# Modulation weights in column halves, attention values by query halves, two late recurrence levels on alternating column groups, and two pieces of sample work in later places, in a one-core decoder layer

## The chip, the cores and the metric

The kernel runs on one core of a Trainium2 chip. The metric is the device time of one execution in microseconds (us), lower is better. The time before is the median of three executions.

## The reference

One layer of a hybrid decoder runs over a prompt of 2048 tokens and over 8 sample rows, all in fp32, width 1024. What matters here, shortened:

```python
mod = c @ w_ada + b_ada                       # conditioning, 9 rows (8 samples and the prompt)
shift, scale, gate = split(mod, 3)
h = rms_norm(x, norm_g) * (1 + scale) + shift
qa, ka, va, za, qb, fb, ib, zb = split(h @ w_in)
# A: attention in a window of 128 keys, two key/value groups, heads of 64
p = softmax(qa @ k.T * d**-0.5 masked to 0 <= rel < 128, with sinks)
ya = (p @ v) * silu(za)
# B: gated linear recurrence over chunks, 4 heads of 128
S_new = exp(Lc) * S + (k * exp(Lc - L)).T @ v
o = (q * exp(L)) @ S + (A = decayed causal q k.T) @ v
yb = rms_norm(o) * silu(zb)
y = g_a * (ya @ w_proj_a) + g_b * (yb @ w_proj_b)
out = x + gate * (y @ w_out)
```

A query sees its own block of 128 keys up to itself and the part of the previous block that is less than 128 keys back. So of the previous block the second half of the queries (64 to 127) needs only keys 64 to 127, and of its own block the first half of the queries (0 to 63) needs only keys 0 to 63.

## The kernel before

The prompt is done in four iterations `it` of 512 tokens. Each is a fixed list `UNITS` of 68 dense units. A unit is one PSUM bank of results, made of 24 matmuls (12 for `pa` and `pb`): each fp32 product is three matmuls of split values (`w_hi` with `h_hi`, `w_hi` with `h_lo`, `w_lo` with `h_hi`). Units alternate between the banks `D0` and `D1`, and a unit has two halves, `hf_` 0 and 1. TensorE (PE) does `dense(it, u, hf_)` and then the side tasks that the table `SIDE` holds for this place, in the order in which `put` and `at_half` wrote them (`at_half(it, n, ..)` is unit n // 2, half n % 2). The other engines go through the same table in the same order. VectorE (DVE) in one half first does "early" tasks (`PV`, `norm` in half 1), then the evacuation of the unit, then the rest. Everything waits by semaphores; the banks `XA` to `XD` are handed round by counts (`full`, `freed`, `free`).

The side tasks that matter here, in an iteration:

- `S`, `norm`, `PT`, `PV` (units 9 to 19): the attention in eight pieces of 128 queries by 2 x 2 heads. `PV` multiplies the transposed weights `PT` by the values `vtok`: for two key blocks and two groups one matmul of 256 columns, results of 64 partitions each. It is 32 bursts in the whole kernel, each recorded as 8 matmuls, since the profile has an fp32 matmul as two.
- `dg` (unit 20): the products of the recurrence in blocks of 32 on the diagonal, 64 matmuls (128 records); DVE then multiplies `qq` by `ff` and takes the diagonal.
- `level` 0 to 6 (from unit 21 on, one per unit): products between blocks of 1, 2, .. 64 tokens. Level 5 is 32 matmuls of 32 result partitions and 32 columns, on column groups 0 and 2 of the array in turn (64 records); level 6 is 16 matmuls of 64 result partitions and 64 columns, all on the first column group (32 records). DVE copies the results to `AT`. `KT`, `o` and `st` follow in units 28 to 31; `KT` waits for DVE's last product of level 6 (`lvl`), `o` for its copy.
- In iteration 1 the sample rows' recurrence: `vB` and `so` (units 1 to 9), `srms` (DVE, unit 26) and `soss` (unit 27): PE transposes what `srms` scaled, and `XC` is used by `soss` and `KT` in turn.
- Five DVE instructions for the sample rows (`esel`, `ib_hi`, `ib_lo`, clearing of `R3`, `qz_b`), called the esel block here, stand before unit 65 of iteration 0 (`NU - 3`) and wait there for the last low part of the next tile (`h_lo` 8).

Ahead of the iterations is the prologue. SyncE (SP) issues all loads on one queue: `w_ada` in eight loads of 128 rows x 2048 columns (shift and scale), the four tiles of x, small rows, then the first three weight blocks. PE multiplies `cT` (the 9 conditioning rows) by the `ada` tiles into four banks (`p_mod` counts pairs of tiles), DVE and ScalarE (ACT) copy the four banks to `mod_rows`, PE turns these rows into columns (32 records of 9 columns, L682), DVE makes `shift` and `gscale`, `modulate` makes h of a tile (8 DVE instructions, L1186), ACT its high part (L942) and GpSimd (POOL) its low part (L1588), and then unit 0 can begin. DVE's order is fixed:

```python
            s.wait_ge("p_mod", 4)
            s.done(cp(mod_rows[:, 0:512], pb["D0"][:, :]), "p_rows")
            s.done(cp(mod_rows[:, 1024:1536], XC[:, :]), "p_rows")
            s.wait_ge("p_T", 3)
```

Of the kernel before, what the change touches and what calls it, by code (L numbers as in the profile page):

```python
# [17 lines left out]
HB = 4  # L18
# [128 lines left out]
put(0, 0, 0, "xturn", 3)  # L147
for it in range(NIT):
# [28 lines left out]
    put(it, 20, 0, "dg", 0, "XA")  # L177
# [26 lines left out]
    if it == 1:  # L204
# [4 lines left out]
        put(1, 27, 0, "soss", 0, "XC")  # L209
# [21 lines left out]
for _it in range(NIT):  # L231
    for _u in UNITS:
        if _u in TH:
# [6 lines left out]
           "lvl", "at0", "smax", "p_exp", "p_norm", "kst", "on", "yf", "yh", "yl", "y7f", "y7h", "y7l", "x_in0", "x_in1", "xst", "rstd",  # L240
# [3 lines left out]
        + [f"ada{k}" for k in range(KT)] + [f"gw{p}" for p in range(4)]  # L244
        + ["p_late", "p_load0", "p_load1", "p_load2", "p_load3", "p_load4", "p_c", "p_T", "p_xs", "p_mod", "p_vec", "p_lb", "p_exp0", "p_rows", "p_scale", "p_x2",
           "p_x3", "p_bg", "fin", "act_step", "dve_step", "pool_step"])

# [51 lines left out]
def build(nc, A, O):  # L299

    ctx = ExitStack()
    with ctx:
# [186 lines left out]
        def _(sp):  # L489
# [10 lines left out]
            def ada_load(k):  # L500
                load(ada[k], A["w_ada"][0, P * k:P * k + P, 0:2 * D], f"ada{k}")

            ada_load(0), ada_load(1)
            load(x_p[0], x[0:P, :], "x_in0")
            load(x_p[1], x[P:2 * P, :], "x_in1")
# [5 lines left out]
            ada_load(2), ada_load(3)  # L511
            load(x_p[2], x[2 * P:3 * P, :], "p_x2")
            load(x_p[3], x[3 * P:4 * P, :], "p_x3")
            for k in range(4, KT):
                ada_load(k)
# [94 lines left out]
            for n in range(NRAW):  # L610
                weights(n)
            load(ones[:, :], A["c_ones"], "p_load2")
# [5 lines left out]
            for p in range(4):  # L618
                s.wait_ge("p_mod", (1, 2, 3, 3)[p])
                load(gate_w[p], A["w_ada"][0, 2 * P * p:2 * P * p + 2 * P, 2 * D:3 * D].rearrange(  # L620
                    "(k p) n -> p k n", p=P), f"gw{p}")
# [24 lines left out]
        def _(pe):  # L646
# [7 lines left out]
            for p in range(4):  # L654
                for k in (2 * p, 2 * p + 1):
                    s.wait_ge(f"ada{k}", 16)
                for n, b in enumerate(("D0", "D1", "XC", "XD")):
                    for k in (2 * p, 2 * p + 1):
                        r = slice(32 * (k % 4), 32 * (k % 4) + 32)
                        ins = mm(pb[b][r, :], cT[:, k, :], ada[k][:, 512 * n:512 * n + 512], start=k < 4, stop=k >= 4)  # L660
                s.done(ins, "p_mod")
                if p == 0:
                    s.wait_ge("p_load1", 16 * 6)
                    s.done(tr(XB[:, 512:512 + NV], vrow, ident[0:NV, 0:NV]), "p_T")
            s.wait_ge("p_vec", 1)
# [11 lines left out]
            s.wait_ge("p_rows", 4)  # L677
            s.wait_ge("p_xs", 1)
            for k in range(KT):
                tr(pb["D1"][:, NS * k:NS * k + NS], xs_row[:, P * k:P * k + P], ident[0:NS, 0:NS])  # L680
            for n in range(2 * KT):
                ins = mm(pb["D0"][:, 9 * n:9 * n + 9], mod_rows[:, P * n:P * n + P], sel, start=True, stop=True)  # L682
            s.done(ins, "p_T")
            x_turn(-1, 2, x_p[2])

            def dense(it, u, hf_):
# [4 lines left out]
                if hf_ == 0:  # L691
                    s.wait_ge(f"D{u % 2}_free", (it * NU + u) // 2)
                    s.wait_ge("w_lo", it * NB + blocks[-1] + 1)
                    if u < NT:
                        s.wait_ge("h_lo", 4 * it + u + 1)
                    if u == 1:
                        s.wait_ge("p_scale", 1)
# [26 lines left out]
            def side(it, task, a, key):  # L724
# [102 lines left out]
                elif task == "dg":  # L827
                    s.wait_ge("kk", 4 * it + 4)
                    s.unit_left(it, "qb", 3)
                    for n in range(16):  # L830
                        h, c = n // NT, P * (n % NT)
                        for g in range(4):
                            r = slice(c + 32 * g, c + 32 * g + 32)
                            ins = mm(bank[32 * g:32 * g + 32, 32 * n:32 * n + 32], kk[:, h, r], qq[:, h, r],
                                     start=True, stop=True)
                elif task == "level":
                    s.wait_ge("lvl", 8 * it + a + 1)
                    w = 2 ** a
                    for n in range(16):
                        h, c = n // NT, P * (n % NT)  # L840
                        for g in range(4) if a < 5 else (0, 2) if a == 5 else (0,):
                            r, left = slice(c + 32 * g, c + 32 * g + 32), 32
# [5 lines left out]
                            ins = mm(bank[32 * g:32 * g + left, m * n:m * n + m], kk[:, h, c + 32 * g:c + 32 * g + left],  # L848
# [69 lines left out]
        def _(act):  # L918
# [24 lines left out]

            s.wait_ge("x_in0", 16)
# [6 lines left out]
            squares(x_p[3], 3, srow[:, :])  # L951
            s.wait_ge("p_lb", 1)
            s.done(fn(lbt[:, 1:3, :], lbt[:, 1:3, :], ACT.Exp), "p_exp0")
            for t in range(NT):
                scale_x(-1, t, x_p[t])
            s.wait_ge("p_mod", 4)
            s.done(fn(mod_rows[:, 512:1024], pb["D1"][:, :], ACT.Copy), "p_rows")
            s.done(fn(mod_rows[:, 1536:2048], XD[:, :], ACT.Copy), "p_rows")
            for n in ATTACH[-1]:
                split_hi(n)  # L960
            h_high(-1, 0)
            h_high(-1, 1)
            h_high(-1, 2)
            h_high(-1, 3)
# [162 lines left out]
        def _(dve):  # L1127
# [53 lines left out]
            def modulate(it, t):  # L1181
                s.full(it, "xT", t)
                s.wait_ge("h_lo", 4 * (it + 1) + t - 1)
# [5 lines left out]

# [504 lines left out]
```

## Time and profile before

| | |
|---|---|
| median of 3 executions | 1648.69 us (1648.18 to 1651.08) |
| profiled execution | 1649.62 us, span of its instructions 1647.8 us |
| PE busy | 1610.2 us, 98% of the span |
| DVE, ACT, POOL busy | 763.6, 594.7, 830.3 us |
| TensorE's mean granted clock | 0.993 of 2.4 GHz |
| bytes moved | 172.6 MB, mean 105 GB/s |

PE is the engine that matters. Its busy time is the sum of times in which any matmul is under way, and a matmul of 512 columns shows as 0.39 us but the next begins 0.23 us after it. So what a burst costs is read from starts, not from sums. DVE, ACT and POOL have slack as averages; what they cost is read where PE waits for them. In the timeline a row is a group of like instructions: start, time from the first's start to the last's end, engine, line, names, partitions x columns, count, and in brackets the idle time before it with what ended it.

### The profile page before, as it was taken

Reading aid. Unit: us, or ns where it says so; the run is one execution under the profiler, and the core shown is the slowest. Engines: PE = TensorE matmul, PEld = TensorE weight load, DVE = VectorE, ACT = ScalarE, POOL = GpSimd, SP = SyncE. Lnnn points to the kernel's source line nnn. Section 1 sums busy time; section 2 is a strip of 40 time slices with the busy share of each in tenths; the row PEclk is TensorE's granted clock in tenths of the full one; section 3 lists DMA queues with packets and bytes.
Section 4 is the critical chain, followed back from the end, with each engine's and each line's share of the span. In section 5 each row is a group of like instructions: output and inputs, shape, how many; then the busy total and the mean of one; then the engine's idle time right before and its main releaser. Section 6 shows DMA issues by size and latency. Waiting matters only on the chain.

```text
span 1647.8 us, 31328 instructions
## 1 busy us (share of the span) xinstructions
PE 1610.2 (98%) x12840; PEld 1297.1 (79%) x12840; DVE 763.6 (46%) x1843; ACT 594.7 (36%) x1160; POOL 830.3 (50%) x1088
## 2 busy tenths in 40 slices
PE   6899999999999999999999999999999999999998
PEld 2687788877878777788878877888888977788887
DVE  2665444323558664522234764623346764633122
ACT  3335423334322551333432354243432354233330
POOL 1624433366664452446666353336677354346671
PEclk9899999999999999999999999999999999999999
DMA  8712212343545331233355232223455232123352
GB/s 315 214 53 85 70 41 65 90 128 105 173 131 131 103 90 35 71 92 114 103 168 139 54 92 63 63 69 115 128 169 162 66 89 66 54 67 88 94 164 72
DMA packets 299848, 172.62 MB, mean 105 GB/s; under 512 B 73646, under 2 KB 290055, under 8 KB 298664
## 3 DMA queue, kind: packets, MB, share of 16 engines
q1 hardware_dynamic: 299704, 170.61, 35.4%
q8 instruction: 102, 1.67, 0.4%
q14 instruction: 42, 0.34, 0.1%
HBM read 159.66 MB, written 11.96 MB: 104 GB/s over the span
## 4 chain that ended last, share of the span: by engine, by line
PE 68%; DVE 2%; issue 1%; ACT 0%; DVEq 0%
PE ps_D L720 39%; PE ps_D L717 18%; PE ps_XB L882 1%; PE ps_XB L876 1%; PE ps_XA L870 1%; PE ps_XB L848 1%; PE ps_XA L848 1%; PE ps_XB L895 1%; PE ps_XA L900 1%; PE ps_XB L894 1%; ACT p_or_hf L1064 0%; DVE p_or_hf L1416 0%; PE ps_XC L887 0%; PE ps_XC L785 0%; PE ps_XD L767 0%
## 5 line engine op out<-in xcount | busy, mean ns | idle before, releaser
L1580 POOL TENSOR_TENSOR w_lo_t<-w_raw,w_hi_t 128x256 fp32r<-128x256 f32 x928 | 680.7, 767 | 657.6 <-ACT w_hi_t L926 657.6
L720 PE MATMUL ps_D<-h_hi_t,w_hi_t 128*128 128x512 f32 x1024 | 415.1, 405 | 0.0
L720 PE MATMUL ps_D<-h_lo_t,w_hi_t 128*128 128x512 f32 x1024 | 401.1, 392 | 0.0
L720 PE MATMUL ps_D<-h_hi_t,w_lo_t 128*128 128x512 f32 x1024 | 400.1, 391 | 0.0
L926 ACT ACTIVATE w_hi_t<-w_raw 128x1024 fp32r<-128x1024 f32 x232 | 240.0, 1052 | 72.3 <-PE ps_D L717 39.3
L720 PEld LDWEIGHTS ps_D<-h_hi_t,w_hi_t 128*128 128x128 f32 x1024 | 192.3, 188 | 58.4 <-issue 21.2
L720 PEld LDWEIGHTS ps_D<-h_hi_t,w_lo_t 128*128 128x128 f32 x1024 | 192.3, 188 | 42.4
L720 PEld LDWEIGHTS ps_D<-h_lo_t,w_hi_t 128*128 128x128 f32 x1024 | 192.6, 188 | 35.8
L717 PE MATMUL ps_D<-w_hi_t,h_hi_t 128*128 128x384 f32 (+1 forms) x384 | 142.2, 370 | 2.7 <-POOL h_lo_t L1588 2.1
L717 PE MATMUL ps_D<-w_hi_t,h_lo_t 128*128 128x384 f32 (+1 forms) x384 | 136.6, 356 | 0.0
L717 PE MATMUL ps_D<-w_lo_t,h_hi_t 128*128 128x384 f32 (+1 forms) x384 | 136.6, 356 | 0.0
L717 PE MATMUL ps_D<-w_hi_t,y_hi_t 128*128 128x512 f32 x256 | 101.7, 397 | 2.1 <-DVE acc_t L1310 2.1
L717 PE MATMUL ps_D<-w_hi_t,y_lo_t 128*128 128x512 f32 x256 | 100.5, 393 | 0.0
L717 PE MATMUL ps_D<-w_lo_t,y_hi_t 128*128 128x512 f32 x256 | 100.3, 392 | 0.0
L989 ACT ACTIVATE th_t<-ps_D,bm_half 128x512 f32<-128x512 f32 x48 | 33.1, 689 | 143.5 <-PE ps_D L720 143.5
L717 PEld LDWEIGHTS ps_D<-w_hi_t,h_hi_t 128*128 128x128 f32 x384 | 72.7, 189 | 14.8 <-issue 8.4
L1292 DVE SCALAR_TENSOR_TENSOR acc_t<-th_t,ps_D 128x512 f32<-128x512 f32 x24 | 16.5, 688 | 140.5 <-PE ps_D L720 140.5
L1064 ACT ACTIVATE p_or_hf<-p_or_hf,sm 128x256 f32<-128x256 f32 x128 | 63.6, 498 | 45.6 <-DVE sm L1400 43.9
L717 PEld LDWEIGHTS ps_D<-w_lo_t,h_hi_t 128*128 128x128 f32 x384 | 72.7, 189 | 5.5
L717 PEld LDWEIGHTS ps_D<-w_hi_t,h_lo_t 128*128 128x128 f32 x384 | 72.8, 190 | 4.6
L1428 DVE SCALAR_TENSOR_TENSOR state<-state,ff,ps_XA 128x128 f32<-128x128 f32 x64 | 18.0, 343 | 117.2 <-PE ps_XA L900 117.2
L1350 DVE TENSOR_TENSOR qq<-qq,ff 128x1024 f32<-128x1024 f32 x28 | 37.6, 1345 | 72.1 <-PE ps_XB L848 45.5
(377 smaller groups left out, 2438.5 us busy)
## 6 DMA issues: line engine op xcount, KB each, us to landing
w_raw<-in_w_in SPq DMA_DIRECT2D x72, 512.0 KB, 3.9
w_raw<-in_w_merge SPq DMA_DIRECT2D x64, 512.0 KB, 4.0
w_raw<-in_w_in SPq DMA_DIRECT2D x64, 256.0 KB, 3.9
w_raw<-in_w_out SPq DMA_DIRECT2D x32, 512.0 KB, 4.1
x_or_AT<-in_x_prompt SPq DMA_DIRECT2D x20, 512.0 KB, 5.4
w_raw<-in_w_proj_a SPq DMA_DIRECT2D x64, 128.0 KB, 2.9
w_raw<-in_w_proj_b SPq DMA_DIRECT2D x32, 256.0 KB, 3.2
xr<-in_x_prompt SPq DMA_DIRECT2D x16, 512.0 KB, 5.1
```

The costliest lines, as they stand in the source:

```text
L717: ins = mm(bank[:, 0:P * nb].rearrange("p (n c) -> p n c", c=P), a[:, k, P * j:P * j + P], w[:, s0:s0 + nb, k, :], start=go, stop=end)
L720: ins = mm(bank[:, :], w[:, s0, k0 + k, :], a[:, k, :], start=go, stop=end)
L848: ins = mm(bank[32 * g:32 * g + left, m * n:m * n + m], kk[:, h, c + 32 * g:c + 32 * g + left], right, start=True, stop=True)
L870: ins = mm(bank[i:i + 32, c:c + 160], qT[r, 2 * mp + m, P * t + i:P * t + i + 32], kT[r, P * t + i:P * t + i + 160], start=True, stop=True)
L876: ins = tr(bank[:, 512 * kt + P * m:512 * kt + P * m + P], p_t[:, m, P * kt:P * kt + P], ident[:, :])
L926: s.done(fn(w_hi[:, SLOT[n % NB]], w_raw[:, n % NRAW], ACT.Copy), "w_hi")
L989: s.leave(fn(dst, bank[:, :], ACT.Tanh, scale=0.5, bias=bm_half[:, c:c + 1]), it, u)
L1064: fn(p_t[:, m, :], p_t[:, m, :], ACT.Exp, bias=negm[:, m:m + 1], accum_out=rsum[:, m:m + 1])
L1292: leave(stt(acc[:, :], thx("ga", j), 1.0, bank[:, :], ALU.add, ALU.mult), it, u)
L1350: s.done(tt(qr, qr, fl[:, :, :, 0:1].broadcast_to(shape), ALU.mult))
L1428: ins = stt(state[:, h, :], state[:, h, :], ff[:, h, P * a:P * a + 1], bank[:, P * h:P * h + P], ALU.mult, ALU.add)
L1580: ins = g_.tensor_tensor(w_lo[:, c, k:k + 2], w_raw[:, n % NRAW, k:k + 2], f32(w_hi[:, c, k:k + 2]), ALU.subtract)
```

## The change

1. `w_ada` is loaded in sixteen loads of half the size. `ada_load(k, 0)` takes columns 0 to 511 of shift and of scale (rows of 2 KB in DRAM in place of 8 KB), and all eight stand after the four x tiles; `ada_load(k, 1)`, the other half, stands after the first three weight blocks. PE's products, the turning of rows and `modulation(h)`, `modulate_half(t, q)`, `h_high_half(t, q)` and the low parts go by halves of the 1024 channels: half 0 of tiles 0 and 1 comes before the second half of `w_ada` is used, and half 0 of unit 0 needs only the first channels.
2. `PV` goes by query halves: for each half the block whose keys it all needs as a matmul of 128 rows and 128 columns, then the other block with 64 rows. Eight matmuls (16 records) of 128 columns in place of four of 256; DVE evacuates in two instructions of 128 columns a partition in place of one of 256.
3. Level 5 and level 6 put consecutive matmuls on different column groups (0, 2, 1, 3 and 0, 1), and DVE's copies become twice as many of half the size.
4. In iterations 1 to 3 `dg` goes head by head in units 17 to 20, and so does DVE's product.
5. `soss` goes from unit 27, half 0, to unit 28, half 1. The esel block goes from before unit 65 of iteration 0 to before unit 0 of iteration 1.

```diff
-put(0, 0, 0, "xturn", 3)
+put(0, 0, 0, "xturn", 2)
+put(0, 0, 1, "xturn", 3)
...
-    put(it, 20, 0, "dg", 0, "XA")
+    if it == 0:
+        put(0, 20, 0, "dg", 3, "XA", (0, "dg", 0))
+    else:
+        for _h in range(HB):
+            put(it, 17 + _h, 0, "dg", _h, "XC", (it, "dg", 0))
...
-        put(1, 27, 0, "soss", 0, "XC")
+        put(1, 28, 1, "soss", 0, "XC")
...
+            def ada_load(k, h):
+                load(ada[k].rearrange("p (s h n) -> p s h n", s=2, h=2)[:, :, h],
+                     A["w_ada"][0, P * k:P * k + P, 0:2 * D].rearrange("p (s h n) -> p s h n", s=2, h=2)[:, :, h], f"ada{KT * h + k}")
...
             for n in range(NRAW):
                 weights(n)
+            for k in range(KT):
+                ada_load(k, 1)
...
+            def ada_half(h):
+                for p in range(4):
                     for k in (2 * p, 2 * p + 1):
...
+            def turn_rows(h):
+                bank, c = ((pb["D0"], 0), (XC, P))[h]
+                for i in range(8):
+                    n = 4 * h + i % 4 + 8 * (i // 4)
+                    ins = mm(bank[:, c + 9 * i:c + 9 * i + 9], mod_rows[:, P * n:P * n + P], sel, start=True, stop=True)
+                s.done(ins, "p_T")
...
+            turn_rows(0)
+            s.wait_ge("p_vec", 1)
+            ada_half(1)
+            s.wait_ge("p_rows", 4)
+            turn_rows(1)
...
+                if it == 0 and u < NT:
+                    s.wait_ge("h_lo", (1, 3, 2, 4, 5, 6, 7, 8)[2 * u + hf_])
...
                             else:
                                 left = m = w
                                 right = qq[:, h, c + 32 * g + w:c + 32 * g + 2 * w]
-                            ins = mm(bank[32 * g:32 * g + left, m * n:m * n + m], kk[:, h, c + 32 * g:c + 32 * g + left],
+                                row, col = 32 * g + w * (n % 2), n // 2
+                            ins = mm(bank[row:row + left, m * col:m * col + m], kk[:, h, c + 32 * g:c + 32 * g + left],
                                      right, start=True, stop=True)
...
-                    for kt in range(2):
-                        for g in range(G):
-                            ins = mm(bank[DH * g:DH * g + DH, 0:256], vtok[:, t + kt, DH * g:DH * g + DH],
-                                     PT[:, kt, 256 * g:256 * g + 256], start=kt == 0, stop=kt == 1)
+                    for own in (True, False):
+                        for i in range(2):
+                            kt, r = (i, slice(0, P)) if own else (1 - i, slice(64 * i, 64 * i + 64))
+                            for g in range(G):
+                                ins = mm(bank[DH * g:DH * g + DH, 512 * i:512 * i + P].rearrange("p (m q) -> p m q", m=2),
+                                         vtok[r, t + kt, DH * g:DH * g + DH],
+                                         PT[r, kt, 256 * g:256 * g + 256].rearrange("p (m i q) -> p m i q", m=2, i=2)[:, :, i],
+                                         start=own, stop=not own)
...
+            modulation(0)
+            modulate_half(0, 0), modulate_half(1, 0)
+            s.wait_ge("p_mod", 8)
+            s.done(cp(mod_rows[:, 1536:2048], XD[:, :]), "p_rows")
+            modulation(1)
+            modulate_half(0, 1), modulate_half(1, 1)
...
                 elif task == "dg":
-                    s.full(*key)
-                    do(tt(qq[:, :, :], qq[:, :, :], ff[:, :, :], ALU.mult), "lvl")
+                    if a < 3:
+                        s.wait_ge("dgp", 3 * (it - 1) + a + 1)
+                        do(tt(qq[:, a, :], qq[:, a, :], ff[:, a, :], ALU.mult))
+                        return
...
-                    if (it, u) == (0, NU - 3):
-                        s.wait_ge("h_lo", 8)
+                    if (it, u) == (1, 0):
+                        s.wait_ge("h_lo", h_tiles(0, 3))
                         s.wait_ge("s_win", 32)
```

What the change moves shows in the order of the instructions on SP, on DVE and on PE. SP's queue in the prologue, before, after four small loads (`x_or_AT` and `s_st_lo` hold x tiles, the other targets of `in_w_ada` are the `ada` tiles):

```order
L493 DMA qq<-in_w_ada 128x2048
L493 DMA ff<-in_w_ada 128x2048
L493 DMA x_or_AT<-in_x_prompt 128x1024 x2
...
L493 DMA s_st_lo<-in_x_prompt 128x1024 x2
L493 DMA silu_za<-in_w_ada 128x2048
L493 DMA ibtok<-in_w_ada 128x2048
L493 DMA s_st_hi<-in_w_ada 128x2048
L493 DMA th_t<-in_w_ada 128x2048
L493 DMA w_raw<-in_w_in 128x8x64 x2
L493 DMA w_raw<-in_w_in 128x8x128 x2
```

The same place now, the last four rows up to the constants:

```order
L503 DMA x_or_AT<-in_x_prompt 128x1024 x2
L503 DMA s_st_lo<-in_x_prompt 128x1024 x2
...
L503 DMA qq<-in_w_ada 128x2x512
...
L503 DMA th_t<-in_w_ada 128x2x512
L503 DMA w_raw<-in_w_in 128x8x64 x2
L503 DMA w_raw<-in_w_in 128x8x128 x2
L503 DMA qq<-in_w_ada 128x2x512
...
L503 DMA th_t<-in_w_ada 128x2x512
L503 DMA ones<-in_c_ones 128x128
```

The x tiles moved ahead of `w_ada`, and the second halves moved behind the weight blocks. DVE at the end of iteration 0, before (`acc_t` and `xr` are the evacuation of an output unit, L1186 the last tile's modulation, L1274 the first unit of iteration 1):

```order
L1186 TENSOR_SCALAR PT_or_qa<-ps_XB,gscale,shift 128x128 x8
L1554 CAST esel_t<-ident 8x1024
L1555 CAST rows_r<-rowsS 8x512
L1556 TENSOR_TENSOR rows_r<-rowsS,rows_r 8x512
L1557 MEMSET PT_or_qa 128x1024
L1558 COPY PT_or_qa<-smS 128x4x8
L1310 TENSOR_TENSOR acc_t<-ps_D,gate_bc 128x512
L1312 TENSOR_TENSOR xr<-xr,acc_t 128x512
...
L1274 TENSOR_TENSOR yf_t<-ps_D,gain 128x128
```

And now:

```order
L1217 TENSOR_SCALAR PT_or_qa<-ps_XB,gscale,shift 128x128 x8
L1361 TENSOR_TENSOR acc_t<-ps_D,gate_bc 128x512
L1363 TENSOR_TENSOR xr<-xr,acc_t 128x512
...
L1616 CAST esel_t<-ident 8x1024
L1617 CAST rows_r<-rowsS 8x512
L1618 TENSOR_TENSOR rows_r<-rowsS,rows_r 8x512
L1619 MEMSET PT_or_qa 128x1024
L1620 COPY PT_or_qa<-smS 128x4x8
L1325 TENSOR_TENSOR yf_t<-ps_D,gain 128x128
```

The block moved behind the evacuations of the last three units, right ahead of the first evacuation of iteration 1. PE in iteration 1, before (L848 is level 6, L822 `soss`, L720 dense, L887 `KT`):

```order
L720 MATMUL ps_D<-h_hi_t,w_lo_t 128x512
L848 MATMUL ps_XB<-qq,kk 64x64 x16
L822 MATMUL ps_XC<-ident,srow 128x128
L720 MATMUL ps_D<-h_hi_t,w_hi_t 128x512
L720 MATMUL ps_D<-h_lo_t,w_hi_t 128x512
...
L887 MATMUL ps_XC<-ident,kk 128x128 x4
```

And now, where it stands a unit and a half later (L921 and L922 are `o`, L927 `st`, L841 `soss`, L914 the next `KT`, of the second tile):

```order
L921 MATMUL ps_XB<-state,qq 128x128
L922 MATMUL ps_XB<-ibtok,x_or_AT 128x128
L927 MATMUL ps_XA<-ibtok,kst_t 128x128 x4
L841 MATMUL ps_XC<-ident,srow 128x128
L739 MATMUL ps_D<-h_hi_t,w_hi_t 128x512
...
L914 MATMUL ps_XC<-ident,kk 128x128 x4
```

`soss` moved from behind level 6 to behind the first `o` and `st`.

## Rows read from the trace of the kernel before

**Rows 1.** The page's first part, and the clock row of its slices.

```profile
PE 1610.2 (98%) x12840; PEld 1297.1 (79%) x12840; DVE 763.6 (46%) x1843; ACT 594.7 (36%) x1160; POOL 830.3 (50%) x1088
...
PEclk9899999999999999999999999999999999999999
```

**Rows 2.** PE's own waits: total us, times, longest.

```profile
PE ps_XA L673 <- DVE p_or_hf L1186: 3.7, 1, 3.7
...
PE ps_XC L822 <- DVE srow L1527: 2.4, 1, 2.4
PE ps_D L717 <- DVE acc_t L1310: 2.1, 1, 2.1
```

**Rows 3.** Timeline of the prologue, 30 to 58 us.

```profile
31.43 0.59 PE L660 MATMUL ps_D<-s_st_hi,cT_or_ab 128*32 128x512 f32 x1 [0.52 <-DMA th_t<-in_w_ada]
...
34.47 0.59 PE L660 MATMUL ps_XD<-th_t,cT_or_ab 128*32 128x512 f32 x1
...
35.17 0.69 DVE L1227 COPY qq<-ps_D 128x512 f32<-128x512 f32 x1 [7.34 <-PE ps_XD L660]
...
37.48 4.38 PE L682 MATMUL ps_D<-misc,qq 128*128 128x9 f32 x32
...
42.84 2.64 DVE L1186 TENSOR_SCALAR p_or_hf<-ps_XA,gscale,shift 128x128 f32<-128x128 f32 x8
45.51 1.06 ACT L942 ACTIVATE h_hi_t<-p_or_hf 128x1024 fp32r<-128x1024 f32 x1 [6.50 <-DVE p_or_hf L1186]
...
46.65 2.77 POOL L1588 TENSOR_TENSOR h_lo_t<-p_or_hf,h_hi_t 128x256 fp32r<-128x256 f32 x4 [1.21 <-ACT h_hi_t L942]
...
49.57 0.66 PE L717 MATMUL ps_D<-w_hi_t,h_hi_t 128*128 128x384 f32 x1 [2.06 <-POOL h_lo_t L1588]
...
57.85 0.44 PE L717 MATMUL ps_D<-w_hi_t,h_hi_t 128*128 128x384 f32 x1
```

**Rows 4.** DMA rate in 40 slices of 1.5 us, 0 to 60 us.

```profile
GB/s 0 69 172 410 426 407 410 409 324 421 415 399 410 448 410 421 415 426 431 333 246 222 302 297 194 23 62 371 423 418 418 412 412 388 328 44 0 0 11 170
```

**Rows 5.** DMA rate in 40 slices of 0.45 us, 1630 to 1648 us.

```profile
GB/s 0 0 0 0 0 0 0 27 364 191 0 0 36 0 0 0 0 0 0 0 360 223 0 0 0 0 0 0 0 0 0 0 319 339 215 143 290 150 0 0
```

**Rows 6.** Timeline at the turn from iteration 0 to 1.

```profile
474.37 1.15 DVE L1554 CAST esel_t<-ident 8x1024 fp32r<-8x1024 f32 x1 [4.10 <-issue]
...
479.75 0.50 PE L717 MATMUL ps_D<-w_hi_t,y_hi_t 128*128 128x512 f32 x1 [2.08 <-DVE acc_t L1310]
...
487.94 0.69 DVE L1312 TENSOR_TENSOR xr<-xr,acc_t 128x512 f32<-128x512 f32 x1
...
498.08 1.13 DVE L1517 SCALAR_TENSOR_TENSOR s_st_hi<-ps_XD,smS,s_st_hi 128x128 f32<-128x128 f32 x4 [1.97 <-POOL s_st_hi L1636]
```

**Rows 7.** Windows view after it: length, busy by engine, granted clock.

```profile
480.70:484.20 3.50, 3.50 (x11) 2.69 (x10) 1.46 (x3) 0.00 (x0) 0.67 (x1) 0.51 0.75 195
```

**Rows 8.** Timeline around `soss`, iteration 1, DVE and PE.

```profile
679.90 0.48 PE L720 MATMUL ps_D<-h_hi_t,w_hi_t 128*128 128x512 f32 x1
...
682.13 0.20 DVE L1353 TENSOR_TENSOR ff<-ff 128x16 f32<-128x16 f32 x1
...
685.47 0.60 PE L887 MATMUL ps_XC<-ident,kk 128*128 128x128 f32 x4
```

**Rows 9.** PE's timeline: bursts `S` and `so`, `PV`, `dg`, level 5, level 6.

```profile
541.41 0.78 PE L870 MATMUL ps_XA<-kT,qT_or_szb 64*32 64x160 f32 x32
542.11 0.43 PE L818 MATMUL ps_XC<-s_st_lo,PT_or_qa 128*32 128x128 f32 x8
...
623.23 1.08 PE L882 MATMUL ps_XB<-PT_or_qa,vtok 128*64 128x256 f32 x8
...
627.23 1.30 PE L834 MATMUL ps_XA<-qq,kk 128*32 128x32 f32 x128
...
668.59 1.21 PE L848 MATMUL ps_XA<-qq,kk 128*32 128x32 f32 x64
...
1072.13 2.08 PE L848 MATMUL ps_XB<-qq,kk 128*64 128x64 f32 x32
```

More of the change, by code:

```diff
@@ L510, in _ @@
             load(vrow[V_OG:NV], A["o_norm_g"], "p_load1")
[L511 to L515, printed above, removed]
+            for k in range(KT):
+                ada_load(k, 0)
             def weights(n):
@@ L611, in _ @@
                 weights(n)
+            for k in range(KT):
+                ada_load(k, 1)
             load(ones[:, :], A["c_ones"], "p_load2")
@@ L841, in side @@
                         for g in range(4) if a < 5 else (0, 2) if a == 5 else (0,):
-                            r, left = slice(c + 32 * g, c + 32 * g + 32), 32
+                            r, left, row, col = slice(c + 32 * g, c + 32 * g + 32), 32, 32 * g, n
                             if a < 5:
@@ L1188, in modulate, with modulate_half, modulation @@
                 free(ins, it, "xT", t)
+            def modulate_half(t, q):
+                s.full(-1, "xT", t)
+                if t >= 2:
+                    s.wait_ge("h_lo", t + 1)
+                bank = pb[BANK[(-1, "xT", t)]]
+                for k in range(4 * q, 4 * q + 4):
+                    ins = ts(hf[t % 2][:, k, :], bank[:, P * k:P * k + P], gscale[:, k, 8:9], shift[:, k, 8:9],
+                             ALU.mult, ALU.add)
+                free(ins, -1, "xT", t) if q else do(ins, "hm")
+            def modulation(h):
+                s.wait_ge("p_T", 3 + h)
+                k = slice(4 * h, 4 * h + 4)
+                bank, c = ((pb["D0"], 0), (XC, P))[h]
+                rows = [bank[:, c + 36 * n:c + 36 * n + 36].rearrange("p (k b) -> p k b", b=9) for n in (0, 1)]
+                b_sh, b_sc, g_n = (vec[:, c0 + 4 * h:c0 + 4 * h + 4].unsqueeze(2).broadcast_to([P, 4, 9])
+                                   for c0 in (V_ADA, V_ADA + KT, V_NG))
+                s.done(tt(shift[:, k, :], rows[0], b_sh, ALU.add))
+                do(tt(gscale[:, k, :], rows[1], b_sc, ALU.add))
+                do(stt(gscale[:, k, :], gscale[:, k, :], 1.0, g_n, ALU.add, ALU.mult))
             s.done(v.memset(hS[:, :, :], 0.0))
@@ L1422, in side @@
                     s.full(*key)
-                    free(stt(yf_slot(16 * it + t)[:, pair], XB[:, 0:256].rearrange("p (m n) -> p m n", m=2), 0.5,
-                             sza[:, pair, P * t:P * t + P], ALU.mult, ALU.mult), *key)
+                    y = yf_slot(16 * it + t)
+                    for i in range(2):
+                        q = slice(64 * i, 64 * i + 64)
+                        ins = stt(y[:, pair, q], XB[:, 512 * i:512 * i + P].rearrange("p (m q) -> p m q", m=2), 0.5,
+                                  sza[:, pair, P * t + 64 * i:P * t + 64 * i + 64], ALU.mult, ALU.mult)
+                    free(ins, *key)
                 elif task == "st":
@@ L1599, in _ @@
                 split_lo(n)
[L1600 to L1601 removed]
+            for n, (t, q) in enumerate(((0, 0), (1, 0), (0, 1), (1, 1), (2, 0), (2, 1), (3, 0), (3, 1))):
+                s.wait_ge("h_hi", n + 1)
+                k, c = slice(4 * q, 4 * q + 4), slice(P * t, P * t + P)
+                s.done(g_.tensor_tensor(h_lo[:, k, c], hf[t % 2][:, k], f32(h_hi[:, k, c]), ALU.subtract), "h_lo")
             for it in range(NIT):
```

112 lines of the change are left out of this document (52 added, 60 removed).

## Prediction

> **What bounds the kernel now.** I read the page's first part and its clock row [rows 1]: PE is busy 98% of the span and granted full clock in nearly every slice. So time can go only where PE waits, where its clock is half, or where a burst between dense matmuls gets shorter. The chain of waits [rows 2] gives the first kind: 3.7 us in the prologue, 2.4 us at `soss`, 2.1 us for `acc_t`; what DVE, ACT and POOL do elsewhere is hidden. So I read three timelines: the prologue, the turn of iterations, and `soss`; then the bursts. The durations are of one profiled execution of 1649.62 us; the median of three, 1648.69, is 0.9 below it, and I take that off at the end.
>
> **Prologue.** Before, PE takes the last pair of `ada` tiles at 31.43 and ends about 35.06 (34.47 + 0.59), and a serial chain follows [rows 3]: copies, 32 transposed records 4.38, DVE's modulation of all channels 2.64, ACT 1.06, POOL 2.77, PE's first dense matmul 49.57, its second half 57.85. That includes a half-clock stretch, since PE had idled. In the DMA row [rows 4] the loads start near 3.3 and run flat at some 415 GB/s to 28.5; that is 10.5 MB (8.4 of `w_ada`, 2.1 of x); then 1.57 MB of weight blocks at 246 to 194, counted as 265 GB/s, 5.9 us. PE took the last tile 2.9 after 28.5.
> Now the queue is x, first half of `w_ada` (4.2 MB), weights, second half (4.2 MB). The half loads have rows of 2 KB. No row shows 128 such rows of loads in a long stream; the kernel's last stores, rows of 2 KB, peak at 360 and 364 GB/s [rows 5]. Between 265 (the weight blocks) and 415 I take 390, nearer to the large loads, which the peaks of a short, half-empty stream reach almost. So 8.4 MB take 21.5, and the last half tile lands at 3.3 + 5.1 (x, 2.1 MB at 415) + 21.5 + 5.9 = 35.8, seen by PE at 38.7. The bytes are the same, but the weights now lie ahead of the end: this is the cost. The gain is the chain behind it: the last pair of half tiles 1.8 (half of 3.63) to 40.5; a copy 0.69 to 41.2; the 16 records of the second half 2.2 to 43.4; the small DVE work on the vectors, 0.98 by the gap between the turning and the modulation in [rows 3], to 44.4; half of DVE's eight modulations 1.32 to 45.7; half of ACT's 1.06 to 46.3 with its start; half of POOL's 2.77 with its start to 47.9. Half 0 of unit 0 has gone by then, so PE begins the second half of unit 0 there: 2.1 for twelve short matmuls, two side bursts of 1.0 (transposes of x tiles and the next), 0.5 for half clock, and the place that is 57.85 before comes at 48.0 + 2.1 + 2.0 + 0.5 = 52.7. **−5.1.** Bounds: at 415 GB/s the landing is 1.3 earlier and half clock may vanish too, −8; at 300 for 8.4 MB it is 6.5 later, which takes all of it: 0. All the extra semaphore steps are in this chain, none elsewhere.
>
> **Esel block.** Before, it begins at 474.37 on DVE (waiting there for the last low part, idle 4.10), and the evacuation `acc_t` behind it makes PE idle 2.08 before 479.75 [rows 6]. Then PE's clock falls: in 480.70 to 484.20 the granted clock is 0.51 of full speed [rows 7], that is 1.2 GHz in place of 2.4, after full-speed work and that idle. 3.5 us at half clock do 1.8 us of work, so 1.7 is lost. Gone both: **−3.7.** The block itself takes about 4.6 and now starts behind the last evacuation of the iteration (487.94 + 0.69 = 488.63) to 493.2. What is queued behind it on DVE is the first `yf_t` of iteration 1 and then its sample work; DVE waited for POOL 1.97 before 498.08 [rows 6], so a delay of about 1.3 is absorbed. If that cover were not there, it would be 1.3 back on PE.
>
> **`soss`.** PE waits 2.38 of the 2.4 for DVE's `srow` [rows 2]. At unit 28, half 1, `srow` is long ready: −2.4. What is late next: `KT` waits for `lvl`, DVE's last product of level 6, and that product stays where it is: 682.13 + 0.20 = 682.33. Before, `KT` came at 685.47, 5.57 after dense work restarted at 679.90 [rows 8]. Now dense restarts 2.4 earlier, and 0.9 more since level 6 is shorter (below): 676.5 + 5.57 = 682.0, so a new wait of 0.3. **−2.1.** `soss` and the next `KT` share `XC`; half a unit (2.8 us) lies between them, and DVE reads `soss` in a short product.
>
> **Bursts.** A burst in [rows 9] costs from its start to the next dense start; what it costs beyond its array work is found from like ones. `so` is 8 records on four column groups, two rounds of 128 columns: 0.43. `PV` is 8 records on two groups of 256 columns, 4 rounds: 1.08. The difference is six rounds of 128 columns: 0.108 each, and a fixed tail of 0.21. For records of 32 columns, where the count sets the time, `dg` gives (1.30 − 0.2) / 128 = 0.0086 each.
> - Level 5: 64 records 1.21. With all four groups in turn, 0.2 + 64 × 0.0086 = 0.75: gain 0.46 × 4 = **−1.8**.
> - Level 6: 32 records 2.08 [rows 9], 0.059 each, one after the other on one group. Two at a time: 0.2 + 0.94 = 1.14: gain 0.94 × 4 = **−3.8**. DVE's copies double in number, but the next reader is `o`, a unit later.
> - `PV`: the query halves save the key blocks that a query doesn't need: four matmuls of 128 rows (4 rounds of 128) and four of 64 rows, which use four tiles of the array at once (2 rounds). 6 × 0.108 = 0.65, tail 0.21. The unknown is what it costs to go from 128-row to 64-row tiles inside the burst, which no row shows alone. `S`, in tiles of 64 rows by 32 columns, starts at 541.41, and the next burst, in another tile shape, at 542.11: 0.70 [rows 9]. Four rounds of 160 columns are 0.55, so 0.15 is left for the change of shape. New burst 0.65 + 0.21 + 0.15 = 1.01: gain 0.07 × 32 = **−2.2**. With no cost of the change, 0.22 × 32 = −6.9. If the four small matmuls don't overlap and each pays the change, 0.43 + 4 × 0.37 + 0.21 = 2.12 in place of 1.08: +33. `S` speaks against that: its 32 records fit in 0.7 only eight at a time, so row tiles do run together.
> The Trainium skill, page "TensorEngine Tiling (Array Packing)", section Key Properties, says that changing the tiling mode, and not merely the tile, drains TensorE. By that rule the change of shape inside `PV` costs something, and the 0.15 left over at `S` agrees; a reader without it would book the full −6.9. Its Gotcha 1 wants different row tiles in different PSUM banks, and the split writes its halves to columns 0 and 512 of `XB`, two banks, so nothing speaks against the overlap.
> - `dg` in iterations 1 to 3: the same 128 records go as 4 bursts of 32. In units 17 and 18 they join `PV` or `S` bursts, 32 × 0.0086 = 0.27 and a change of shape 0.15; in units 19 and 20 it is a burst with a tail, 0.27 + 0.2 each. Sum 0.42 + 0.42 + 0.47 + 0.47 = 1.78 against 1.30: **+1.4** for three. No PE wait is due to `dg` [rows 2], so DVE's shorter product returns nothing.
>
> **Sum.** −5.1 − 3.7 − 2.1 − 1.8 − 3.8 − 2.2 + 1.4 = −17.3. Own execution 1649.6 − 17.3 = 1632.3; the median 1648.7 − 17.3 = 1631.4; I write 1631.5.
>
> **The rivals.** (A) The change of tile shape costs nothing inside `PV`: −6.9 in place of −2.2, 1626.8. For it: the 0.15 is a remainder of an estimate of rounds; against: it is there. (B) The prologue gives nothing, since short rows and the weights ahead push the last half tile to 42: 1636.6. For it: weight loads at 265 GB/s with their shorter rows [rows 4]; against: the peaks of 360 [rows 5]. (C) The other side: the small `PV` matmuls run one after another with a drain each, +33 in place of −2.2: about 1667. It decides from 1.55 a burst on (15.1 of other gains / 32 = 0.47 above 1.08). For it: level 6 shows 0.059 a record where two matmuls follow on one tile; against: `S`. (D) New waits take most: DVE has 16 more evacuation instructions of `PV` per iteration and twice the copies, and POOL's and DVE's work of the sample rows is later; if `KT`, `o` or an evacuation is late by 1 in a dozen places, 1644. For it: `KT` is down to the edge [rows 8]; against: DVE is busy 46% [rows 1] and only three waits of over 2 are in [rows 2].
>
> **How the numbers follow.** A difference below 0.2%, 3.3 us, is what a measurement of this kernel cannot tell from none. Main case 0.55, A 0.2, B 0.15, D 0.05, C 0.05. All but C are faster by more than 3.3, and I leave 0.03 of D's neighbourhood for the same: faster 0.92, same 0.03, slower 0.05. The main case's own range is 1624 to 1638 (prologue −8 to 0, `PV` between). The range 1623 to 1640 takes in A and B and leaves out C and D.
>
> **What the profile after will show.** `PV` rows of 16 records near 1.01; 0.86 for A, over 1.55 for C. Level 5 near 0.75, level 6 near 1.14. PE's first dense matmul of unit 1 near 52.7; the last DMA slice at full rate ending near 36, later than 40 for B. No wait for `acc_t` and no slice at half clock at the turn of iterations 0 and 1. No wait at L841, and at most 0.3 at the following `KT`. Wrong I would be if a large wait of PE for DVE, POOL or a DMA appears in the chain that isn't named here, or if `PV` bursts come out over 1.3.

## The result and the profile after

The changed kernel takes 1640.23 us (median of five, 1637.64 to 1642.62) against 1651.08 for the kernel before in the same session: ratio 0.9937, interval 0.9926 to 0.9948, some 10.4 us faster by the ratio. The forecast was 17.3 faster and 1631.5, with a range of 1623 to 1640. The profiled execution took 1640.34, span 1638.5, against 1647.8: 9.3 less. So the sign held, and some 7 us of the gain are missing (7.7 between the two traces).

The page of the changed kernel, as [rows 1], with the queue that brings PE's instructions:

```profile
PE 1602.0 (98%) x13096; PEld 1293.9 (79%) x13096; DVE 762.2 (47%) x1900; ACT 595.2 (36%) x1163; POOL 832.3 (51%) x1080
...
PEclk9999999999999999999999999999999999999999
...
q8 instruction: 104, 1.70, 0.4%
```

PE's waits after, as [rows 2]:

```profile
PE ps_XA L871 <- issue: 2.7, 3, 1.7
PE ps_XC L914 <- DVE ff L1409: 1.7, 1, 1.7
PE ps_XC L837 <- issue: 1.6, 1, 1.6
PE ps_XB L871 <- issue: 0.9, 1, 0.9
PE ps_D L736 <- POOL h_lo_t L1665: 0.9, 1, 0.9
```

The waits for `acc_t` and for `srow` are gone. In their place stand three that I had not listed at this size: inside the level bursts (L871), at `KT` (L914) and at the second `so` (L837). "issue" means that the profile names no releaser.

The prologue, as [rows 3]:

```profile
40.33 0.59 PE L671 MATMUL ps_D<-s_st_hi,cT_or_ab 128*32 128x512 f32 x1 [1.56 <-DMA th_t<-in_w_ada]
...
43.09 1.95 PE L678 MATMUL ps_XC<-misc,qq 128*128 128x9 f32 x16 [0.85 <-DVE qq L1284]
...
49.07 0.44 PE L736 MATMUL ps_D<-w_hi_t,h_hi_t 128*128 128x384 f32 x1 [0.91 <-POOL h_lo_t L1665]
...
53.23 0.45 PE L736 MATMUL ps_D<-w_hi_t,h_hi_t 128*128 128x384 f32 x1
```

The last half tiles come at 40.33 and unit 1 begins at 53.23 in place of 57.85: −4.6. The DMA row, 0 to 60 us, as [rows 4]:

```profile
GB/s 0 69 213 404 371 400 262 326 389 401 391 385 388 357 242 218 291 285 332 335 399 404 389 385 385 326 296 280 408 421 410 412 403 389 201 147 212 218 216 208
```

The 2 KB rows run at 385 to 404 where nothing else is mixed in (390 was taken).

The bursts, as [rows 9]: `PV`, a quarter of `dg`, level 5, level 6.

```profile
610.04 1.04 PE L907 MATMUL ps_XB<-PT_or_qa,vtok 128*64 128x128 f32 x16
...
614.85 0.46 PE L853 MATMUL ps_XC<-qq,kk 128*32 128x32 f32 x32
...
663.45 0.76 PE L871 MATMUL ps_XA<-qq,kk 128*32 128x32 f32 x64
...
669.83 1.15 PE L871 MATMUL ps_XB<-qq,kk 128*64 128x64 f32 x32
```

These are 1.04, 0.76 and 1.15 where 1.01, 0.75 and 1.14 were forecast.

The turn of the iterations, POOL and DVE, as [rows 6]; the esel block is 480.67 to 485.69:

```profile
480.35 4.05 POOL L1642 TENSOR_TENSOR w_lo_t<-w_raw,w_hi_t 128x256 fp32r<-128x256 f32 x4 [3.58 <-ACT w_hi_t L953]
480.67 0.36 SPq L503 DMA_DIRECT2D out_dram<-xr  x1
480.67 1.11 DVE L1616 CAST esel_t<-ident 8x1024 fp32r<-8x1024 f32 x1
...
484.43 1.00 SPq L503 DMA_DIRECT2D w_raw<-in_w_in  x2
...
485.47 2.45 SPq L503 DMA_DIRECT2D s_st_hi<-in_state_hgrn  x4
...
489.74 1.05 POOL L1700 TENSOR_TENSOR s_st_hi<-s_st_hi,smS 128x512 f32<-128x512 f32 x1 [2.02 <-DMA s_st_hi<-in_state_hgrn]
...
490.93 1.12 DVE L1579 SCALAR_TENSOR_TENSOR s_st_hi<-ps_XD,smS,s_st_hi 128x128 f32<-128x128 f32 x4 [2.25 <-POOL s_st_hi L1700]
...
492.15 0.43 PE L837 MATMUL ps_XC<-s_st_hi,PT_or_qa 128*32 128x128 f32 x8 [1.62 <-issue]
```

This is to be read backwards. PE waits 1.62 for DVE, DVE 2.25 for POOL, POOL 2.02 for the landing of the recurrent state; SP issues that load at 485.47, behind a `w_raw` load that waited for POOL's group of low parts to end (480.35 + 4.05 = 484.40). Such a group takes 2.97 or 2.80 without the block beside it. And the windows view of 494 to 498, as [rows 7], shows 0.59 of 2.4 GHz after this wait, most of the window at 1.2 GHz:

```profile
494.00:498.00 4.00, 4.00 (x16) 0.59 1.26 258
```

`KT` and the DVE and POOL rows that it waits for, as [rows 8]:

```profile
675.59 3.94 POOL L1642 TENSOR_TENSOR w_lo_t<-w_raw,w_hi_t 128x256 fp32r<-128x256 f32 x4 [3.90 <-ACT w_hi_t L953]
675.80 1.76 DVE L1407 TENSOR_TENSOR kk<-kk,ff 128x1024 f32<-128x1024 f32 x1
677.60 0.59 DVE L1409 TENSOR_TENSOR ff<-ff 128x16 f32<-128x16 f32 x1
...
678.33 0.63 PE L914 MATMUL ps_XC<-ident,kk 128*128 128x128 f32 x4 [1.69 <-DVE ff L1409]
```

Before, the DVE product took 1.22 and the `ff` one 0.20 (POOL was idle there); beside POOL's group they take 1.76 and 0.59, and POOL's group 3.94 for 2.8.

To say where the time went I set the starts of the same dense matmuls of both traces against each other (a negative number is a gain of the changed kernel):

```
prologue                                              -4.6
levels 5 and 6, four iterations       4 x (-.44 -.93)  -5.5
PV, by bursts                               32 x -.05  -1.5
dg, iterations 1 to 3                         3 x .42  +1.3
esel block: wait and half clock gone                   -4.0
  wait at the second so, with half clock               +2.4
soss: wait gone                                        -2.4
  wait at KT                                           +1.9
pauses of PE inside bursts, after minus before        about +4
others (norm transposes, small differences)           -1.2
sum                                                    -9.6
```

The pauses themselves are 4.0 after and 0.7 before, 3.3 more. By the start of the next dense matmul the five bursts with a pause are 4.4 later; the rest is no idle time of PE in the trace.

A pause inside a burst looks like this. It stands before the last of the 128 records of level 1, iteration 0:

```profile
222.44 0.18 PE L871 MATMUL ps_XA<-qq,kk 128*32 128x16 f32 x1 [1.70 <-issue]
```

The DMA packets of the trace show what happens there: the instruction queue of PE moves blocks of 16 KB (q8 above: 104 packets, 1.70 MB; PE's matmuls, weight loads and semaphore instructions in the trace are 26573, or 103.8 times 256), and one such packet begins 2.39 us before the end of this pause. The changed kernel has five pauses like it, 1.70, 0.36, 0.66, 0.92 and 0.37, and each ends 2.3 to 2.7 us after the start of such a packet. The kernel before has one, 0.69. No semaphore is in it. And their place in the stream of instructions is always the same: counted from PE's first instruction in the trace (which is 0; matmuls, weight loads and semaphore instructions), the five stand at numbers 4033, 5058, 10946, 17858 and 23490, and each of these is a multiple of 256 plus 193 or 194. The one of the kernel before stands at 22978, again a multiple of 256 plus 194. So a pause stands where one block of 256 instructions ends. Most such borders are passed without a pause: in the bursts of 128 matmul records (256 instructions with their weight loads) all pauses stand among the last 45 instructions, and some borders there show none.

### The profile page after: what moved, and what is told of

Same layout as the page of the kernel before. It is cut to its first block, busy times and chain, and to the rows that moved or that the text cites. A ratio compares the mean times of both kernels' runs of the same rounds, so it can differ in the third digit from the quotient of the medians.

```text
span 1638.5 us, 31905 instructions
## 1 busy us (share of the span) xinstructions
PE 1602.0 (98%) x13096; PEld 1293.9 (79%) x13096; DVE 762.2 (47%) x1900; ACT 595.2 (36%) x1163; POOL 832.3 (51%) x1080
## 4 chain that ended last, share of the span: by engine, by line
PE 93%; DVE 3%; SPq 2%; issue 1%; DMA 1%; ACT 1%; POOL 0%; DVEq 0%
PE ps_D L739 53%; PE ps_D L736 24%; PE ps_XB L907 2%; PE ps_XB L899 2%; PE ps_XD L792 2%; SPq L503 2%; PE ps_XA L893 1%; PE ps_XB L871 1%; PE ps_XB L922 1%; PE ps_XA L927 1%; PE ps_XB L921 1%; PE ps_XC L804 1%; PE ps_XA L871 1%; DMA th_t<-in_w_ada 1%; PE ps_XC L914 0%
```

## The experiments

**The position of the blocks.** The edit is shown for e2, in the prologue where PE waits for loads; e1 has 16 transposes, e3 48, and e4 puts 32 into the kernel before:

```diff
+            for _ in range(32):
+                tr(XD[:, 128:128 + NV], vrow, ident[0:NV, 0:NV])
             s.done(tr(XD[:, 0:NV], vrow, ident[0:NV, 0:NV]), "p_T")
```

> The changed kernel with 16 more transposes on PE in the prologue, where PE waits for the loads of w_ada (the extra results are not read); they push every later PE instruction back by 64 instructions (the instruction queue of PE moves blocks of 16 KB, 256 instructions). Theory F (instruction fetch): in the changed kernel five pauses of 0.36 to 1.70 us (4.0 in all) inside the level bursts and one dense unit lie 2.3 to 2.7 us behind the start of an instruction fetch, against one of 0.69 before; where a block border falls in a burst of 256 records decides them, so they move to other bursts or vanish: their sum changes by more than 1 us and the time with it (1636 to 1642). Rival G: the pauses belong to their place (data transfers, semaphores): units 22, 82 and 143 keep theirs, sum 4.0, same time within 1 us.

> As e1_shift64 with 32 extra transposes, 128 instructions, half a block. Theory F: the borders fall half a block further; the sum of pauses inside level bursts is different from 4.0, and different from e1's. Rival G: sum 4.0, the same units.

> As e1_shift64 with 48 extra transposes, 192 instructions; p_vec is about 4 us later but has slack. Theory F: again another set of pauses; over the four positions the time spreads by 2 us or more. Rival G: sum 4.0, the same units.

> The kernel before with 32 extra transposes in the prologue, 128 instructions. Theory F: its one pause of 0.69 us at unit 202 moves or goes, and others appear; the time changes by up to 4 us. Rival G: the same 0.69 in unit 202 and the same time.

> The changed kernel itself once more, beside the others on one chip. Theory F with position: pauses inside level bursts near the ones of its first profile (units 22, 82, 143; 4.0 in all), and 3 to 4 us above the e2_shift128 family. Rival: the pauses are chance and differ from its first profile, with the time near 1636.

These texts, and the names of the runs, count a transpose as four instructions. The traces record it as two, one weight load and one matmul. The page of e1 has 16 more of each than the changed kernel's 13096:

```profile
PE 1604.7 (98%) x13112; PEld 1297.5 (79%) x13112; DVE 767.0 (47%) x1900; ACT 595.9 (36%) x1163; POOL 832.9 (51%) x1080
```

So the shifts are 32, 64 and 96 instructions, an eighth, a quarter and three eighths of a block. The "units" 22, 82, 143 and 202 in them are counts of dense matmuls divided by 24: they are level 1 of iterations 0, 1 and 3, and for 143 level 2 of iteration 2.

The runs come from several sessions. The kernel before had a median of 1649.26 beside e1 to e4, 1647.90 beside e5 to e8, 1649.68 beside e9 to e12 and 1649.80 beside f1 to f3. Totals of different groups are therefore compared by their ratios, where an interval is some 2 us to either side, and single causes are read at their place in the traces.

Measured:

| kernel | median us | ratio, interval | pauses in bursts, us |
|---|---|---|---|
| changed | 1640.23 | 0.9937, 0.9926 to 0.9948 | 4.0 |
| changed, again (e12) | 1639.32 | 0.9936, 0.9923 to 0.9948 | 3.6 |
| 16 transposes (e1) | 1637.76 | 0.9930, 0.9917 to 0.9942 | 1.0 |
| 32 transposes (e2) | 1635.94 | 0.9915, 0.9901 to 0.9928 | 0.7 |
| 48 transposes (e3) | 1636.72 | 0.9919, 0.9906 to 0.9933 | 0 |
| before, 32 transposes (e4) | 1648.35 | 0.9994, 0.9985 to 1.0003 | 0 |

More transposes, and less time. The changed kernel again has its pauses in the same bursts, but for one:

```profile
222.50 0.18 PE L871 MATMUL ps_XA<-qq,kk 128*32 128x16 f32 x1 [1.92 <-issue]
```

So position decides, and chance adds to it: 0.7 in e2 was absent in e6, whose PE instructions are the same. e1's only pause is in a burst that has one in the changed kernel too, so this one run would not exclude rival G. But e2's stands in another burst, e3 has none, and every pause in every trace of this case stands at a multiple of 256 plus 193 or 194 (17858 in e1, 17601 in e2), whatever matmul that is. Rival G is out. e1's profiled execution also held a wait of 3.49 at `so` in place of 1.62, which is no pause of this kind: its first recurrent state took 6.06 us to land in place of 4.20. The change brought PE's instructions to a bad position; that is no property of its parts.

**The esel block and the wait at `so`.**

```diff
-                    if (it, u) == (1, 0):
+                    if (it, u) == (0, NU - 3):
```

> e2_shift128 with the esel block back before unit 65 of iteration 0; the rest as changed. In the traces of the changed kernel and of e2 the block in its new place runs beside a group of POOL's low parts (4.05 us in place of 2.97), behind which SP's loads of the recurrent states are issued; PE then waits 1.62 us at the second sample product and 3.5 us at half clock follow. Theory N (new wait): the old place brings back the wait of 2.1 at acc_t with its half clock (4.0 in all) and takes the wait at the sample product back to 0.8 without half clock (2.4 in all): 1635.9 + 1.6 = 1637.5. Rival O (as predicted, the new place is free of cost): 1635.9 + 3.7 = 1639.6, and the wait at the sample product stays at 1.6.

1636.54, ratio 0.9931 (0.9919 to 0.9944), 2.6 us above e2 by the ratios, which can't tell N from O. In the traces, e5 loses 2.2 at `acc_t` and gets 0.4 back at `so`, where the wait is 1.24: 1.8 in all. O, for which the wait stays at 1.6, is out. N's sum of 1.6 is near, with some luck: it booked a half clock on either side, and these cancel. So of the 1.62 at `so` 0.78 was there before the change, 0.4 comes with the block's new place, and for the last 0.5 no run names a cause. Of the half clock neither was right: after a wait of 2.04 here e5 has none, as the windows view (474.2 to 478.2 and 492.5 to 496.5) shows.

```profile
474.20:478.20 4.00, 4.00 (x18) 1.00 0.54 144
492.50:496.50 4.00, 4.00 (x27) 1.00 1.24 276
```

```diff
-            later.setdefault(NU, []).append(("sst", 0, 0))
+            later.setdefault(NU - 1, []).append(("sst", 0, 0))
+            later.setdefault(NU, []).append(("sst", 0, 1))
...
-                    for b in range(NS):
+                    for b in range(2 * a, (NS if a else 2)):
```

> e2_shift128 with the first two loads of recurrent states one place earlier in SP's queue, ahead of the last w_raw loads that wait for POOL. Theory N: the wait of 1.6 us at L839 (second sample product) goes or falls under 0.3, no half clock follows, 2.4 to 3 us less: about 1633.2. Rival: the wait is DVE's own lateness behind the esel block, then it stays and the time is 1635.9.

1632.35, ratio 0.9904 (0.9889 to 0.9919), 1.8 below e2 by the ratios. The wait is 0.34 (L840 is that `so`), and the trace gains 1.3 there:

```profile
488.60 0.43 PE L840 MATMUL ps_XC<-s_st_hi,PT_or_qa 128*32 128x128 f32 x8 [0.34 <-issue]
```

POOL's group beside the block is still 4.06 long; only the load no longer queues behind it. So it was the queue behind POOL, not DVE itself. This mend takes away the part of the wait that was there before the change as well.

**The wait at `KT`.**

```diff
-        put(1, 26, 1, "srms", 0)
-        put(1, 28, 1, "soss", 0, "XC")
+        put(1, 27, 1, "srms", 0)
+        put(1, 29, 1, "soss", 0, "XC")
```

> e2_shift128 with srms (13 small DVE instructions, 4.1 us) from unit 26 to unit 27, half 1, behind DVE's products for level 6, and soss from unit 28 to unit 29, half 1. Theory: PE's wait of 1.69 us for lvl at the first KT of iteration 1 is there because DVE does srms ahead of that product, stretched by POOL's work beside it; it goes: 1635.9 - 1.7 = 1634.2. Rival: the wait is due to level 6 being shorter and the copies being more, so at least 0.6 of it stays.

1633.65, ratio 0.9910 (0.9897 to 0.9924), 0.8 below e2 by the ratios. The wait is gone from the list and the dense work behind it is 1.9 earlier, with nothing left: the rival, that 0.6 stays, is out. With the 4.1 us of `srms` away the shorter level 6 and the doubled copies cost no wait. And without POOL's group beside them the two DVE products take 1.21 and 0.20 again.

**The price of `PV`.** e8 puts the old `PV` back; e9 and e10 are as follows (e10 also has `start=True, stop=True` on what is left, and so leaves out the second key block):

```diff
-    kt, r = (i, slice(0, P)) if own else (1 - i, slice(64 * i, 64 * i + 64))
+    kt, r = (i if own else 1 - i), slice(0, P)
```

```diff
-                    for own in (True, False):
+                    for own in (True,):
```

> e2_shift128 with PV as before: four matmuls of 256 columns, one evacuation of 256. Each burst 1.06 by its row and 1.106 in added cost against 1.058 with query halves: +0.05 x 32 = +1.5, 1637.4. If the half evacuations on DVE cost more elsewhere, the time is the same or lower than 1635.9. The PE stream is 256 instructions shorter in all, so pauses at instruction fetches may come out elsewhere, up to 2 us; the burst rows are what decides.

> e2_shift128 with the second block of PV also in matmuls of all 128 rows (the weights outside of the window are zero), so no change of tile shape inside the burst, but 8 rounds of 128 columns for 6. If the change of shape costs about 0.15 and a round 0.108, the burst costs 0.86 + 0.2 = 1.06, the same as now; without a cost of the change the present burst would be 0.2 shorter than this one. Total 1635.9 within 1.

> e2_shift128 leaving out the second key block of PV (the four matmuls of 64 rows), so the attention result is incomplete. It prices them: 1.06 - (0.43 + 0.2) = 0.43 a burst of which 0.22 are the two rounds and 0.2 the change of shape. If the change is free: burst 0.84.

1637.65 (0.9935, 0.9922 to 0.9947), 1636.02 (0.9917, 0.9903 to 0.9930) and 1623.56 (one execution). The first `PV` burst of iteration 0 in e9 and e10 (L909):

```profile
120.85 1.09 PE L909 MATMUL ps_XB<-PT_or_qa,vtok 128*64 128x128 f32 x16
```

```profile
121.19 0.66 PE L909 MATMUL ps_XB<-PT_or_qa,vtok 128*64 128x128 f32 x8
```

What a burst adds between two dense matmuls, median of the lone bursts: old `PV` 1.105, 128 rows 1.116, now 1.058, own half alone 0.679. From 4 rounds at 0.679 to 8 at 1.116 a round is 0.109. The four 64-row matmuls cost 0.379: two rounds 0.218, and 0.16 for the change of tile shape. Could it be that the small matmuls simply don't run side by side? The single records of the trace say no. In the burst at 610.04 above, the eight small records start in two sets of four, at 610.625 to 610.645 and at 610.785 to 610.805. The step from the last 128-row pair (610.415) to the first set is 0.21 where a round is 0.109, and the step between the two sets is 0.16. The gain of the split is 0.05 a burst, where it would be 0.2 without that. e8's total says little: it is 3.3 above e2's by the ratios, and 3.4 in the traces, of which 1.5 is a half clock behind `so` that e2's profiled execution has not, and 1.5 the bursts.

**The order of the prologue's loads.** `ada_load(k, 1)` ahead of `weights(n)`:

> e2_shift128 with the second half of w_ada ahead of the first three weight blocks in SP's queue, as the whole of w_ada was before. Theory L (the place behind the weights sets the start of the second half of unit 0): PE has the last half tile 6 us earlier, but the weight blocks land at 38 and ACT and POOL need 6.2 us for their parts after that, in front of the low parts of h in POOL's order; unit 1 begins at 55 or later, 2 to 5 us slower than now. Rival: the weight blocks have slack and the prologue gets 3 us shorter.

1637.56, ratio 0.9926 (0.9913 to 0.9938). PE has the last half tile at 34.27, yet the second rows can only be turned at 42.64, since ACT's copy of them stands behind its high parts of the late weight blocks:

```profile
34.27 0.59 PE L671 MATMUL ps_D<-s_st_hi,cT_or_ab 128*32 128x512 f32 x1 [0.89 <-DMA th_t<-in_w_ada]
...
42.64 3.58 PE L678 MATMUL ps_XC<-misc,qq 128*128 128x9 f32 x16 [6.46 <-ACT qq L994]
```

The turning itself ran at half clock there, 3.58 in place of 1.95. First dense work begins at 47.0 in place of 44.0 in e2, and unit 1 at 55.59 in place of 52.72. Theory L, with the price at its place, 2.9, in its range; the totals are only 1.8 apart by the ratios.

**Together.** f1 is e2 with both mends, f2 also undoes the split of `dg`, f3 is f1 without the extra transposes.

> e2_shift128 with both mends, the state loads of e6 and the srms place of e7. If the causes add: wait at the sample product 0.3, none at KT, 1635.9 - 1.3 - 1.9 = 1632.7, or 1631 where e2's runs hold some half-clock stretches; ratio to before about 0.9895. If the one mend takes the other's cover (a new wait of PE elsewhere): as e6 or e7, 0.990 to 0.991.

> f1_both_mends with dg in one burst in unit 20 of all iterations, and one DVE product, as before. By its bursts the split costs 0.42 an iteration, 1.3 in all: this is 1.3 faster. If the split frees DVE for level 0 (its wait is not seen in any trace): the same or slower.

> f1_both_mends without the 32 extra transposes, so that PE's instructions stand where the changed kernel has them. Theory F: the pauses of 1.7 to 1.9 at unit 22, about 0.5 in unit 26, 0.6 to 0.9 in 143 and 0.4 in 202 are back: 3 to 4 us above f1. If they were chance or due to the waits that were mended: as f1.

| kernel | median us | ratio, interval |
|---|---|---|
| f1 | 1630.77 | 0.9882, 0.9868 to 0.9895 |
| f2 | 1629.11 | 0.9872, 0.9859 to 0.9886 |
| f3 | 1636.36 | 0.9918, 0.9905 to 0.9932 |

The mends add: f1's trace is 3.5 shorter than e2's. The pauses come back with the position, 4.6 us in f3 against 0.9 in f1, at the same numbers in the stream but for one. f3 is 5.6 slower in the same session, more than the 3 to 4 expected; by the starts of dense matmuls 4.5 of it is at the bursts with pauses and 0.5 in the prologue:

```profile
222.82 0.18 PE L872 MATMUL ps_XA<-qq,kk 128*32 128x16 f32 x1 [2.05 <-issue]
```

`dg` in one burst is 1.7 faster in the medians and 0.5 an iteration in the trace: its split is a loss. (f2 also lacks f1's pause of 0.9, so the medians alone don't price it.) f2 is the fastest, 0.9872 of before.

## Why the prediction was wrong

The missing 7 us are the pauses (about 4), the longer wait at `so` with its half clock (2.1 over the forecast of the esel block's net gain), the wait at `KT` (1.6), `PV` (0.7) and the prologue (0.5), less small gains that I had not counted. The pauses are the largest item, and the sum had no term for them; with the stream in another position the same change gave 1635.94 (e2).

- **Prologue, −5.1: right, −4.6.** The last half tile came at 40.3 for 38.7, 1.6 late, because the weight blocks and the start of the second half ran at 218 to 335 GB/s for a longer stretch. From there to unit 1 it was 12.9 in place of 14.0: the half clock that I had added (0.5) did not come in this execution, and the rest of the chain was 0.6 shorter than costed.
- **Esel block, −3.7: the step "a delay of about 1.3 is absorbed" failed.** DVE's own delay was not what counted. The block slows POOL's group beside it by 1.1, SP's loads stand behind that group, and PE, which is 8 us earlier here, waits longer for the recurrent state: 1.62 in place of 0.78, of which 0.4 goes with the block's place (e5). I had read DVE's idle time as slack, though it waited there for POOL, which waited for a load. e6 shows it: with the load out of that queue the wait is gone. The other half of the mistake is the 1.7 for half clock: after waits like this one, half clock comes in some executions and not in others (below), so it was not a sure cost of before. The kernel before itself, with 32 transposes ahead (e4), waited 2.02 at `acc_t` with no half clock after it (the clock reads 0.95 of 2.4 GHz in all its records), and its next half unit was 1.6 earlier. And it came back behind the new wait in the profiled execution. Net −1.6.
- **`soss`, −2.1: the step "a new wait of 0.3" was undersized, 1.7.** 0.4 is from DVE's doubled copies of level 5 and 0.9 from the DVE products, stretched because PE's earlier work brought POOL's group beside them. I had carried DVE's times over as fixed. Net −0.5. On page "Trainium Architecture — The Big Picture" of the Trainium skill, the section on what this means for kernel authors, DVE and GpSimd are said to contend for a shared port pair; both directions are seen here (1.22 to 1.76 and 2.8 to 3.9).
- **Level 5 and 6, −1.8 and −3.8: right.** −0.44 and −0.93 each. Column groups in turn do work side by side.
- **`PV`, −2.2: right in kind, −1.5.** The change of tile shape costs 0.16 (0.15 taken), a round 0.109; the tail is a little longer. The rule of the Trainium skill in "TensorEngine Tiling (Array Packing)", section Key Properties, says that a change of tiling mode drains TensorE. The 0.16 from e9 and e10 agrees with it.
- **`dg`, +1.4: right, +1.3,** and nothing returned (f2).
- **What was not in the sum:** the pauses at instruction fetches, 4.0 against 0.7. Rival D spoke of new waits in a dozen places at evacuations and `KT`; in kind it was nearest, in place it was wrong, since the largest item has no semaphore. (It also counted 16 more evacuations of `PV` per iteration; there are 8.) The kernel before showed one pause of this kind, 0.69, in its waits view as "issue", which I had passed over.

## What to carry to other kernels

When work is moved behind an idle stretch of an engine, ask what that engine was idle for: a chain of waits through another engine and a load queue is no slack. Count as a cost of moved work what it does to the engine beside it, here VectorE against GpSimd, and to the queue behind that one. Differences of some 0.2% between two kernels with dense bursts of short matmuls can be the position of the instruction stream alone: test with a few dozen extra instructions ahead, at a place where the engine waits anyway, before believing a part to be good or bad.

## What the runs showed of the hardware that was not expected

- PE stops for 0.3 to 2.1 us, nearly always inside bursts of 128 short matmul records, and each stop ends 2.3 to 2.9 us behind the start of a 16 KB instruction packet. In all traces of this case it stands at the same place of a block of 256 instructions (193 or 194 from PE's first), and in the bursts always among their last 45 instructions. 32, 64 or 96 instructions ahead change the sum from 4.0 to between 0 and 1.0. That the block was not there in time is what the packets suggest; no run shows PE's own view of it.
- Half clock (1.2 in place of 2.4 GHz) after a short idle isn't settled by its length: a wait of 1.53 to 1.72 us at the same `so` was followed by it in the changed kernel, again in e12, in e8 and e11, but not in e2 (1.63), e9 (1.67) or e3 (1.79), nor behind 1.91 in e7. At `acc_t` it came behind 2.08 in the kernel before, and not behind 2.04 in e5 or 2.02 in e4. It costs 1.5 to 1.7 us when it comes. What decides it stays open.
